# Stage boundaries worked by halves of the tokens, and input squares summed on VectorE

## The reference, cut to what matters

```
x = x + w * post_norm(f(pre_norm(x)))      # w = 1/2 for ffn, 1 for the mixers hg and gd
_rmsnorm(v) = v * rsqrt(mean(v*v over the 1024 features) + 1e-6) * gain
ffn:  f(h) = (silu(h @ w_gate) * (h @ w_up)) @ w_out        # 1024 -> 2 x 2816 -> 1024
hg:   HGRN2 recurrence, projections 1024 -> 4096, back from 1024
gd:   gated DeltaNet, projections 1024 -> 6 x 1024 (+ 32 columns), back from 2048
```

## Time and profile before

| | |
|---|---|
| median of three runs | 2353.21 us |
| profiled execution, its own time | 2352.79 us |
| its span, first to last instruction | 2351.1 us |
| matmul busy (PE) | 2274.0 us, 97% |
| VectorE (DVE) busy | 1239.0 us, 53% |
| ScalarE (ACT) busy | 982.3 us, 42% |
| GpSimd (POOL) busy | 422.4 us, 18% |
| mean granted TensorE clock | 0.987 |

### The profile page before, as it was taken

How to read it: one execution, slowest core, us unless ns; L and a number is a source line. 1 busy time by engine, 2 the same in 40 slices (tenths; PEclk the granted TensorE clock), 3 DMA queues, 4 the chain that set the end, 5 groups by cost and what they waited for, 6 DMA issues and landing times.

```text
span 2351.1 us, 31330 instructions
## 1 busy us (share of the span) xinstructions
PE 2274.0 (97%) x11226; PEld 1855.6 (79%) x11226; DVE 1239.0 (53%) x1490; ACT 982.3 (42%) x1403; POOL 422.4 (18%) x323
## 2 busy tenths in 40 slices
PE   8999998999999999999999998899999999999999
PEld 7888886788778888878888886677788887888887
DVE  5445336666555454345545338776655644645423
ACT  5322334555543223334232336565566643432312
POOL 2112101111122121012212002123721102112100
PEclk9999999999999999999999999899999999999999
DMA  5333332222223332332332332122112222443341
GB/s 163 106 89 91 90 96 71 81 75 76 63 63 115 90 98 79 97 101 90 98 98 74 104 90 91 48 72 64 60 58 82 64 90 72 117 115 90 104 146 63
DMA packets 84719, 207.92 MB, mean 88 GB/s; under 512 B 25088, under 2 KB 29312, under 8 KB 84640
## 3 DMA queue, kind: packets, MB, share of 16 engines
q1 hardware_dynamic: 84640, 206.85, 29.1%
HBM read 202.56 MB, written 4.26 MB: 88 GB/s over the span
## 4 chain that ended last, share of the span: by engine, by line
PE 87%; DVE 6%; ACT 3%; POOL 2%; issue 1%; DMA 0%; DVEq 0%; SPq 0%; ACTq 0%; POOLq 0%
PE bank L1787 68%; PE bank L2031 7%; PE bank L1837 5%; DVE h_lo L1067 1%; POOL gd_o L1710 1%; DVE resid L1082 1%; DVE w_lo L1063 1%; POOL sq L1707 1%; DVE y L1077 1%; PE bank L2193 1%; PE bank L2200 1%; ACT w_hi L571 0%; ACT h_hi L595 0%; PE bank L1992 0%; PE bank L2172 0%
## 5 line engine op out<-in xcount | busy, mean ns | idle before, releaser
L1063 DVE TENSOR_TENSOR w_lo<-raw,w_hi 128x1024 fp32r<-128x1024 f32 x395 | 571.8, 1465 | 513.6 <-ACT w_hi L571 513.4
L1787 PE MATMUL bank<-h_hi,w_hi 128*128 128x512 f32 x1720 | 685.3, 398 | 38.8 <-DVE h_lo L1067 32.1
L1787 PE MATMUL bank<-h_hi,w_lo 128*128 128x512 f32 x1720 | 675.7, 393 | 0.0
L1787 PE MATMUL bank<-h_lo,w_hi 128*128 128x512 f32 x1696 | 666.1, 393 | 0.0
L571 ACT ACTIVATE w_hi<-raw 128x1024 fp32r<-128x1024 f32 x395 | 415.4, 1055 | 563.4 <-PE bank L1787 470.0
L1787 PEld LDWEIGHTS bank<-h_hi,w_hi 128*128 128x128 f32 x1720 | 326.8, 190 | 116.4 <-issue 33.2
L1787 PEld LDWEIGHTS bank<-h_hi,w_lo 128*128 128x128 f32 x1720 | 326.4, 190 | 69.7
L1787 PEld LDWEIGHTS bank<-h_lo,w_hi 128*128 128x128 f32 x1696 | 322.4, 190 | 68.7 <-issue 3.1
L1651 POOL TENSOR_TENSOR y<-y,up 128x512 f32<-128x512 f32 x88 | 173.1, 1967 | 744.2 <-DVE up L1106 670.1
L1106 DVE TENSOR_TENSOR up<-bank,rms 128x512 f32<-128x512 f32 x88 | 60.7, 690 | 351.3 <-PE bank L1787 351.3
L1787 PE MATMUL bank<-act_hi,w_hi 128*128 128x512 f32 x528 | 205.4, 389 | 0.0
(11 more groups left out here) (277 smaller groups left out, 2632.5 us busy)
## 6 DMA issues: line engine op xcount, KB each, us to landing
raw<-in_ffn_in SPq DMA_DIRECT2D x172, 512.0 KB, 3.7
raw<-in_gd_in SPq DMA_DIRECT2D x49, 512.0 KB, 3.6
raw<-in_ffn_out SPq DMA_DIRECT2D x48, 384.0 KB, 3.1
raw<-in_hg_in SPq DMA_DIRECT2D x32, 512.0 KB, 3.6
raw<-in_ffn_out SPq DMA_DIRECT2D x48, 320.0 KB, 2.9
raw<-in_last_out SPq DMA_DIRECT2D x22, 512.0 KB, 3.6
raw<-in_gd_out SPq DMA_DIRECT2D x16, 512.0 KB, 3.7
raw<-in_hg_out SPq DMA_DIRECT2D x8, 512.0 KB, 3.5
```

The costliest lines, as they stand in the source:

```text
L1063: nc.vector.tensor_tensor(w_lo[:, r, :], raw[:, r, :], w_hi[:, r, :].bitcast(f32), ALU.subtract).then_inc(lo_split, 1)
L1787: ins = nc.tensor.matmul(dst, w, moving[ml][:, k, :], start=first and n == 0 and (wl, ml) == (0, 0), stop=last and n == len(ks) - 1 and wl ...
```

## The change

The output tiles 0 to 6 stay as they are. The last one is made in two halves of 256 tokens, in two banks (7 and 6), and each half has a sum of its own, of two float32 matmuls with 256 columns, and a root of its own. The sum of half 0 stands on TensorE behind the first two blocks of half 1 (6 matmuls); the sum of half 1 stands in the next stage, behind chunk 0, half 0, of units 0 and 1. VectorE's boundary list has 12 items: chunks 0 to 3 for the first half, chunks 0 to 3 for the second, chunks 4 to 7 whole. `head_start` has the same order; the 48 matmuls of chunks 0 to 3 become 96 of 256 columns. The `w_lo` splits of units 0 to 3 move into VectorE's boundary list, one before each of its first items. The squares of the new x go to a tile of their own, `x_sq`, and VectorE adds them up itself with seven adds (`gather`) behind the 12 items; GpSimd does this only for stage 0. The sum of the input norm is then one float32 matmul of 512 columns instead of two. In hg and gd it stands behind all of `head_start`, in ffn behind unit 4 (the one that goes to bank 5). VectorE's and ScalarE's lists of the ffn pairs are as before.

```diff
+        ITEMS = [(c, 0) for c in range(SPLIT)] + [(c, 1) for c in range(SPLIT)] + [(c, 2) for c in range(SPLIT, KD)]
...
             def pre(s):
...
+                    high(s, 2)
+                    high(s, 3)
+                    root(post_sums(s - 1, 1), 1, half(1))
+                    for i in range(SPLIT, N_ITEMS):
+                        high(s, i)
+                        square(i - SPLIT)
                 split((first_unit[s] + RING, 0))
-                root(2 * s)
+                root(pre_sums(s), 0, half(2))
...
+                act.wait_ge(half_made, s + 1)
+                act.wait_ge(acc_done, POOLED * (2 * s + 1) + POOLED - 1)
+                last_half(0)
+                root(post_sums(s, 0), 1, half(0))
+                if n_u == 4:
+                    split((w0 + 1, 0))
+                high(s + 1, 0)
+                if n_u > 1:
+                    split((w0 + 2, 0))
+                high(s + 1, 1)
+                act.wait_ge(unit_used, w0)
+                last_half(1)
+                split((w0 + 3, 0))
...
+                def gather(c):
+                    dve.wait_ge(sq_done, SQUARES * s + c + 1)
+                    wait(dve, acc_done, POOLED * 2 * s + c - 1)
+                    nc.vector.tensor_tensor(acc[:], x_sq[:, 0, :] if c == 1 else acc[:], x_sq[:, c, :], ALU.add).then_inc(acc_done, 1)
+                split((first_unit[s], 0))
                 scale(0)
                 add(0)
...
+                for i in range(N_ITEMS):
+                    if i < RING - 1:
+                        split((first_unit[s] + i + 1, 0))
+                    if i + 1 < N_ITEMS:
+                        scale(i + 1)
+                    low(s, i)
+                    if i + 1 < N_ITEMS:
+                        add(i + 1)
+                for c in range(1, KD):
+                    gather(c)
...
+                for i in range(SPLIT - 1):
+                    for q in range(RING - 1):
+                        chunk(i, q)
+                        if i == 0 and q == 1:
+                            sum_outputs(s - 1, 1)
+                for i in range(SPLIT - 1):
+                    chunk(i, RING - 1)
+                for i in range(SPLIT - 1, N_ITEMS):
                     for q in range(RING):
-                        ins = blocks(bank[q][:], (u0 + q, 0), k, (h_hi, h_lo), [k], k == 0, k == KD - 1)
...
+                        chunk(i, q)
+                if kinds[s] != "ffn":
+                    sum_inputs(s)
...
                         blocks(bank[banks[q]][:], u, 0, (h_hi, h_lo), range(KD), True, True).then_inc(unit_used, 1)
+                        if s and banks[q] == 5:
+                            sum_inputs(s)
...
+                def last_tile(u):
+                    alone = 1 if n_u == 4 else 0
+                    turns = [(q, h) for q in range(alone) for h in range(2)] + [(q, h) for h in range(2) for q in range(alone, n_u)]
+                    for q, h in turns:
+                        pe.wait_ge(lo_split, u + q + 1 + SKEW)
+                        ks = range(cuts[q], cuts[q + 1])
+                        dst = bank[7 - h][:]
+                        if (q, h) == (alone, 1):
+                            blocks(dst, (u + q, 0), 0, moving, ks[:2], q == 0, False, h)
+                            sum_outputs(s, 0)
+                            ins = blocks(dst, (u + q, 0), 2, moving, ks[2:], False, q == n_u - 1, h)
```

More of the change, by code:

```diff
@@ L585, in pre, with root @@
-            def pre(s):
[L586 to L594, removed]
+            def root(n, which, cols):
+                act.wait_ge(sum_ready, n)
+                nc.scalar.activation(rms[:, which, cols], bank[4][:, cols], ACT.Ln, bias=eps, scale=1.0 / D).then_inc(rms_logged, 1)
+                act.wait_ge(rms_logged, n)
+                nc.scalar.activation(rms[:, which, cols], rms[:, which, cols], ACT.Exp, scale=-0.5).then_inc(rms_ready, 1)
@@ L651, in out_tiles @@
                 tiles = RING // n_u
+                per = max(tiles, 2)
                 v0 = first_unit[s] + IN_UNITS[kinds[s]]
[L654 to L669, removed]
@@ L670, in out_tiles, with tile @@
-                step = max(tiles, 2) // tiles
+                def tile(i, t):
+                    u = (v0 + t * n_u, 4 * i) if not isinstance(i, int) else (v0 + 4 * i + t * n_u, 0)
+                    c = tiles * i + t
+                    for q in range(n_u - 1):
+                        split(ahead(u, 4 + q))
+                    act.wait_ge(unit_used, count(u) + n_u)
+                    wait(act, acc_done, POOLED * (2 * s + 1) + c - 1)
+                    nc.scalar.activation(sq[:, t % 2, :], bank[t % 2][:], ACT.Square).then_inc(sq_done, 1)
+                    wait(act, y_scaled, N_ITEMS * s)
+                    nc.scalar.activation(m[:, bass.ds(c, 1), :].rearrange("p a n -> p (a n)"), bank[t % 2][:], ACT.Copy).then_inc(m_copied, 1)
+                    split(ahead(u, 3 + n_u))
@@ L671, in out_tiles, with last_half @@
+                def last_half(h):
+                    nc.scalar.activation(sq[:, POOLED % 2, half(h)], bank[7 - h][:, half(h)], ACT.Square).then_inc(sq_done, 1)
+                    nc.scalar.activation(m[:, KD - 1, half(h)], bank[7 - h][:, half(h)], ACT.Copy).then_inc(m_copied, 1)
+                step = per // tiles
                 n = KD // tiles
                 act.preload_act_table_set("natural_log_exp_and_others")
-                with act.Fori(0, n - step, step) as i:
-                    four(i)
@@ L675, in out_tiles @@
-                four(n - step, s == LAST - 1)
-                root(2 * s + 1)
+                if n > 2 * step:
+                    with act.Fori(0, n - step, step) as i:
+                        for t in range(per):
+                            tile(i, t)
+                else:
+                    for t in range(per):
+                        tile(0, t)
+                for t in range(per - 1):
+                    tile(n - step, t)
+                w0 = first_unit[s + 1]
+                for q in range(RING - n_u, RING - 3):
+                    split((w0 + q, 0))
@@ L1063, in split, with low @@
                 nc.vector.tensor_tensor(w_lo[:, r, :], raw[:, r, :], w_hi[:, r, :].bitcast(f32), ALU.subtract).then_inc(lo_split, 1)
[L1065 to L1068, removed]
-            def boundary(s):
[L1072 to L1082, removed]
+            def low(s, i):
+                c, h = ITEMS[i] if s else (i, 2)
+                dve.wait_ge(h_hi_ready, items_before(s) + i + 1)
+                nc.vector.scalar_tensor_tensor(out=h_lo[:, c, half(h)], in0=x[:, c, half(h)], scalar=pre_gain(s, c),
+                                               in1=h_hi[:, c, half(h)].bitcast(f32), op0=ALU.mult, op1=ALU.subtract).then_inc(h_ready, 1)
@@ L1869, in out_proj, with four @@
                 v0 = first_unit[s] + IN_UNITS[kinds[s]]
-                def four(i, peeled=False):
+                def four(i, peeled=False, last=False):
                     for t in range(max(tiles, 2)):
@@ L1876, in four @@
                         c = tiles * i + t
+                        if last and t == max(tiles, 2) - 1:
+                            last_tile(v0 + t * n_u + 4 * i)
+                            continue
                         if not peeled or t >= 2:
-                            pe.wait_ge(m_copied, KD * s + c - 1)
+                            pe.wait_ge(m_copied, COPIES * s + c - 1)
                         for q in range(n_u):
```

155 lines of the change are left out of this document (102 added, 53 removed).

## The result

The changed kernel takes 2364.08 us (median of five runs, 2361.11 to 2368.89) against 2351.65 us before (2350.95 to 2354.58): a ratio of 1.0050, 95% interval 1.0035 to 1.0065. It is slower by about 12 us. The profiled execution has a span of 2362.3 us, 11.2 more than before.

The account below looks back on a forecast made before the run. TensorE holds 87% of the chain of waits; boundary waits and slow clock total 38.3 us, the most to gain. Terms +9.5 + 3.6 - 4.0 + 0.8 = +9.9 on 2352.79 gave 2362.5 us, range 2350 to 2373 for 8 in 10.

Parts of the forecast that it names:

- Halves at 0.120: On TensorE, a 256-column matmul takes 0.120 us, so each pair costs 0.0133 us more than a whole one.
- The wait of 4.69 goes: At a boundary's first chunk, work after half 0 covers its root in ffn or gd tiles; hg keeps 2.1 us.
- Waits in the head, 2.5: TensorE waits 2.5 us in all in each boundary's head, 4.6 at boundary 2, as VectorE's items come late.
- Unit 4, 1.7: In ffn stages, unit 4's w_lo stands behind the seven gathers on VectorE, so TensorE waits 1.7 us.
- Unit 5, 4.15: In ffn stages, unit 5's w_lo stands behind gate and up, which need the input root: TensorE waits 4.15 us.
- Unit 6, 1.2: In ffn stages, unit 6's w_lo ends 11.54 us after the sum, unit 5 at 10.45: a wait of 1.2 us.
- Slow clock, +3.6 beyond the wait at unit 6: In three ffn stages, half clock after unit 5's wait costs 1.2 us each beyond unit 6's wait, +3.6 together.
- hg and gd, -2.0 each: In stages hg and gd, the input norm's Exp comes at 29.9 us after the last tile, not 31.96: -2.0 each.
- Covered root: Rival at unit 5 of ffn stages: its w_lo does not wait for the input root, 2343 us; chance 0.11.
- Dear halves: Rival on half matmuls: at 0.188 us each a pair costs 0.149 more, +57, 2419 us; chance 0.05.
- Even: Rival: no clock fall at unit 5 nor longer in hg, halves cost 0.1075; 2354 us, chance 0.2.
- those for h_lo fall from 32.1 to about 14: Sign to watch: TensorE's total waits for VectorE's h_lo fall from 32.1 us to about 14.

Follow-up runs that it names:

- e1: Changed kernel with the input norm's sum in ffn stages moved from behind unit 4 to behind the whole head: 2340.74 us, ratio 0.9955 to the kernel before.
- e7: e1 with the last out-projection tile whole again (512 columns), the boundary's chunks still in halves: 2359.05 us, ratio 1.0032 to the kernel before.
- e3: Changed kernel with three of the seven gathers moved between VectorE's last whole chunks: 2360.88 us, ratio 1.0036 to the kernel before.
- e2: Changed kernel with unit 5's w_hi and w_lo made before the wait for the root in stages 2, 3, 5: 2366.45 us, ratio 1.0060 to before.
- e4: e1 with the seven gather adds put back on GpSimd: 2363.41 us, ratio 1.0042 to the kernel before.
- e5: Changed kernel with the edits of e1 and e3 together: 2338.97 us, ratio 0.9946 to the kernel before.
- e8: e6 with hg's unit 4 w_lo split ahead of VectorE's wait for the input root: 2338.61 us, ratio 0.9941 to the kernel before.
- e6: e5 with w_lo of head units already there split before VectorE's first chunk operation: 2335.33 us, ratio 0.9932 to the kernel before.

## Why the prediction was right, step by step

The forecast was 2362.5 us and slower, +9.9; measured are 2364.08 and +12.4 by the medians, +11.2 between the profiles. (The terms and the 2352.79 make 2362.7, not 2362.5.) I take the starts of the last tiles (the half 0 sums less 90, 30 or 54 matmuls of 0.12) to split the 11.2:

| stretch | forecast | measured |
|---|---|---|
| stage 0 | 0 | +0.7 |
| boundary 1 and hg | -1.2 | -3.4 |
| boundary 2 (hg to ffn) and stage 2 | +5.2 | +5.5 |
| boundary 3 and stage 3 | +4.1 | +3.5 |
| boundary 4 and gd | -2.0 | -0.6 |
| boundary 5 and stage 5 | +3.8 | +5.4 |

The mechanism, two new waits per ffn stage that eat up the gain of the boundary, is shown by e1 and e7. That the sum of the terms comes so close is in part luck: the rows are off by up to 2.2 us either way, and what was forecast too high in the heads and at unit 6 stands against slow clock that was not forecast.

The forecast counts a wait between the starts of matmuls, while the profile's idle time begins where the record before ends, which is 0.16 us later (0.28 against 0.120; 0.39 against 0.2267). Below, "by starts" is the forecast's own measure.

- *Halves at 0.120.* Measured 0.120. The fixed 0.0133 us on top of the columns was the right reading, and the float32 rows' 0.1075 the wrong one. The rule of the Trainium skill ("TensorE: Matmul & The Clock Gate", "Back-to-back issue gap", 262 cycles or 0.109 us for 256 columns) is not what this trace shows, which has 0.120.
- *The wait of 4.69 goes.* Shown by the trace, and by e7 as the work of the half tile. Boundary 2's remainder: 2.1 forecast, 1.87 measured, 2.0 by starts.
- *Waits in the head, 2.5.* Measured 1.4; by starts 2.0 at boundary 3: 0.1, 1.1, 0.35 and 0.45 at items 1, 2, 3 and the first whole chunk, where 0.2, 1.2, 0.5 and 0.6 were forecast. Each is some 0.1 us too high; why is open.
- *Unit 4, 1.7.* Measured 1.76 to 1.79, 1.9 by starts; e3 shows the gathers as its cause.
- *Unit 5, 4.15.* Measured 3.90, 4.06 by starts; e1 shows that the place of the sum is its cause, and e2 that it is the whole chain behind the root.
- *Unit 6, 1.2.* There is no such wait. Its w_lo ended 11.51 us after the sum's start in stage 2 (703.40 to 714.91), as forecast (11.54), but unit 5 ran at half the clock and was longer for it by 2.5 us in stage 2, 1.6 in stage 3 and 2.7 in stage 5, each more than the 1.2. The forecast knew that the two overlap, but left 1.2 us of it as a wait and counted only the rest as slow clock.
- *Slow clock, +3.6 beyond the wait at unit 6.* The two terms had 7.2 us together, and behind unit 5 the slow clock cost 6.8: the windows last 6.8, 3.4 and 6.8 us, and the first 3.5 us of them, in sum, fell into the waits. What the forecast lacked is one more window of 3.4 us in stage 5, behind unit 4's wait of 1.79: 1.7 us more.
- *hg and gd, -2.0 each.* In hg, unit 4 starts at 407.27 instead of 408.42, with the 0.7 of stage 0 a gain of 1.9. A further 1.5 is a slow piece of 3.4 us at 443 in the kernel before that the changed one lacks. In gd the first unit behind the head also gains 1.9 (1443.15 to 1447.61, with the tile 6.3 late), and some 1.3 are lost later, where the changed kernel's profile has 6.8 us more at 0.50. Neither the 1.5 nor the 1.3 was forecast, and no run here shows that the change causes them. In hg the window of slow clock at unit 4's wait of 6.52 us lasts 10.2 us, against 3.4 in the kernel before, yet the 0.8 put down for it did not show: from unit 4 to the next wait, at 442.83 and 441.68, both kernels take 34.41 us.

Of the rivals, Covered root failed for the changed kernel at the point named, the order of VectorE's list. Its own price was half right. It asked only that the w_lo of unit 5 not wait for the root, and had 2343 for that. e2 makes just this edit, and the wait moved to unit 6: 2366.45. e1, where the root itself comes earlier, has 2340.74. In that price the forecast had overlooked the chain that stands behind the root, up to the split of unit 6. Dear halves and Even fell with the 0.120 and the slow clock.

One reading of mine was loose: I gave all 32.1 us of the earlier trace rows to the boundaries, and 7.3 of it belong to the start of stage 0. The sum didn't use that number, but the sign "those for h_lo fall from 32.1 to about 14" did. At the boundaries 8.7 are left, so the total of 16.4 does not confirm it.

## What to carry to other kernels

When a reduction is moved behind other work to spare its wait, list everything that stands behind its result on every engine's list, down to the split of the unit after next: here two lines' move cost 23 us, since a whole drain, silu, product and split chain hung on the root. A serial stretch between two phases hides well behind half of the last tile, and the halves cost only the fixed part of each matmul once more (0.0133 us here). The wait that is left can have a second price in the clock that follows it, so read both from the trace of a wait of like length.

## What was not expected of the hardware

A single wait of 1.79 us before unit 4 in stage 5 was followed by 3.4 us at a granted clock of 0.52, while the same wait at 697.83 and at 1072.02 (1.78 and 1.76) was not. Waits of 3.9 us were followed by 6.8, 3.4 and 6.8 us. The clearest case is a wait in stage hg that no edit touches:

```profile
442.83 0.77 PE L1787 MATMUL bank<-h_hi,w_hi 128*128 128x512 f32 x1 [2.25 <-DVE q_in L1258]
```

```profile
441.68 0.47 PE L1861 MATMUL bank<-h_hi,w_hi 128*128 128x512 f32 x1 [2.26 <-DVE q_in L1322]
```

The first is from the kernel before, the second from the changed one. All ten profiles have this wait of 2.25 or 2.26 us. In six (before, e1, e4, e5, e7, e8) the clock was at 0.50 for 3.4 us with it, in four (the changed kernel, e2, e3, e6) it was not. The gd stage, which the edits hardly touch, had some 31 and 37 us at 0.50 in the profiles of the two kernels. So two profiles can differ by some microseconds through the clock alone, and the runs of the changed kernel lie 7.8 us apart where those of the kernel before lie 3.6 apart.

An add of GpSimd delays VectorE's operations of 256 columns as much as those of 512: they grow from 0.48 to 1.5 us in e4, so halving operations makes this contention dearer by share.
